# Router scores by token in one product, and a shift shared by two engines

## The reference, cut to what matters

```python
hp = modulate(xp, norm2_g[l], mp[3], mp[4])      # rmsnorm(x) * (1 + scale) + shift
...
scores = jax.nn.sigmoid((t @ router_w).astype(jnp.float32))       # 384 tokens x 16 experts
sel = scores + router_bias.astype(jnp.float32)
...
hid = swiglu(jnp.einsum('td,edf->tef', t, w_in))
routed = jnp.einsum('tef,efd->td', hid * gates[..., None].astype(hid.dtype), w_out)
shared = swiglu(t @ sh_in) @ sh_out
```

## Time and profile before

| what | us |
|---|---|
| median of three runs | 1160.81 |
| lowest and highest of them | 1158.30, 1163.59 |
| the profiled execution | 1160.04 |
| its span in the trace | 1158.2 |

### The profile page before, as it was taken

The page is one execution under the profiler, slowest core; times in us unless marked ns, Lnnn a source line. Parts: engine busy times, 40 slices in busy tenths (PEclk is TensorE's granted clock), DMA queues, the critical chain, the costliest instruction groups (busy, mean ns, idle before and its releaser), DMA issues.

```text
span 1158.2 us, 16832 instructions
## 1 busy us (share of the span) xinstructions
PE 1065.1 (92%) x5726; PEld 835.6 (72%) x5726; DVE 674.9 (58%) x1124; ACT 644.0 (56%) x1155; POOL 312.5 (27%) x265
## 2 busy tenths in 40 slices
PE   5899998899899999999799999978878989999997
PEld 1785654446857888887499999957767976778885
DVE  1432663434355999996565640177766134798994
ACT  2523432445245887886555452398775424588880
POOL 0520920003202000001436655655556600100000
PEclk9899999999988999999899999998898999899999
DMA  9643527993139999995323333476630304999973
GB/s 385 237 182 145 200 109 284 423 420 132 64 114 358 411 411 411 411 409 199 140 73 113 110 111 143 148 214 188 189 119 1 145 1 161 378 412 410 411 311 128
DMA packets 86368, 266.71 MB, mean 230 GB/s; under 512 B 7329, under 2 KB 39585, under 8 KB 73249
## 3 DMA queue, kind: packets, MB, share of 16 engines
q1 hardware_dynamic: 78496, 243.30, 55.6%
q0 software_dynamic: 2880, 12.58, 2.9%
q10 hardware_dynamic: 4928, 10.01, 2.4%
HBM read 245.68 MB, written 15.47 MB: 225 GB/s over the span
## 4 chain that ended last, share of the span: by engine, by line
PE 71%; ACT 8%; DMA 8%; DVE 7%; POOL 3%; issue 2%; SPq 0%; ACTq 0%; POOLq 0%; DVEq 0%
PE bank L2117 16%; PE bank L2118 16%; PE bank L2119 16%; PE bank L2141 3%; PE bank L2401 3%; POOL wlo L736 2%; PE bank L2203 2%; ACT seg L1349 2%; PE bank L2659 2%; DMA h_blk<-h_rows,tok_of 2%; DMA modb<-modb 1%; PE bank L2376 1%; ACT whi L883 1%; DMA rowb<-acs_rows 1%; DMA modw<-wide_mods 1%
## 5 line engine op out<-in xcount | busy, mean ns | idle before, releaser
L736 POOL TENSOR_TENSOR wlo<-raw,whi 128x512 fp32r<-128x512 f32 x152 | 201.0, 1356 | 264.7 <-ACT whi L883 258.9
L2117 PE MATMUL bank<-hhi,whi 128*128 128x384 f32 (+1 forms) x504 | 176.9, 351 | 12.9 <-DVE hlo L1471 9.5
L2118 PE MATMUL bank<-hlo,whi 128*128 128x384 f32 (+1 forms) x504 | 173.3, 344 | 0.0
L2119 PE MATMUL bank<-hhi,wlo 128*128 128x384 f32 (+1 forms) x504 | 173.0, 343 | 0.0
L1849 DVE TENSOR_TENSOR wlo<-raw_more,whi 128x1024 fp32r<-128x1024 f32 x108 | 128.7, 1222 | 14.4 <-ACT whi L1146 12.9
L1849 DVE TENSOR_TENSOR wlo<-raw,whi 128x1024 fp32r<-128x1024 f32 x108 | 128.2, 1221 | 10.3 <-ACT whi L1146 8.1
L1146 ACT CAST whi<-raw_more 128x1024 fp32r<-128x1024 f32 x108 | 111.5, 1049 | 29.6 <-PE bank L2119 25.4
L1146 ACT CAST whi<-raw 128x1024 fp32r<-128x1024 f32 x108 | 111.5, 1053 | 22.6 <-PE bank L2119 12.3
L2117 PE MATMUL bank<-whi,blk_hi 128*128 128x512 f32 x288 | 115.1, 400 | 0.0
L2118 PE MATMUL bank<-wlo,blk_hi 128*128 128x512 f32 x288 | 113.8, 395 | 0.0
L2119 PE MATMUL bank<-whi,blk_lo 128*128 128x512 f32 x288 | 113.7, 395 | 0.0
(11 more groups left out here) (355 smaller groups left out, 1996.6 us busy)
## 6 DMA issues: line engine op xcount, KB each, us to landing
raw<-stream SPq DMA_DIRECT2D x56, 1024.0 KB, 4.8
raw<-experts SPq DMA_DIRECT2D x108, 512.0 KB, 11.4
raw_more<-experts SPq DMA_DIRECT2D x108, 512.0 KB, 11.3
modw<-wide_mods SPq DMA_DIRECT2D x37, 1024.0 KB, 12.5
rowb<-acs_rows SPq DMA_DIRECT2D x48, 256.0 KB, 5.2
shared<-shared SPq DMA_DIRECT2D x6, 1024.0 KB, 6.1
h_next<-h_blk SPq DMA_DIRECT2D x9, 512.0 KB, 10.6
y_rows<-y_sb ACTq DMA_DIRECT2D x9, 512.0 KB, 6.7
```

Source lines behind the costliest of these rows:

```text
L736: ins = pool.tensor_tensor(wlo[:, q % SPL, w], raw[:, pos % RAW, w], whi[:, q % SPL, w].bitcast(F32), ALU.subtract)
L2117: pe.matmul(dst, whi_, xhi_, start=first, stop=False)
L2118: pe.matmul(dst, whi_, xlo_, start=False, stop=False)
L2119: return pe.matmul(dst, wlo_, xhi_, start=False, stop=last)
```

## The change

The job `router` and its result are gone. The job `scores` now does the router's products the other way round: for each chunk of 128 features and each of the three tiles of 128 tokens, the tokens (128 x 128 of `hn`) are stationary and the router's weights (16 columns) are moving. The 24 products gather in one bank as 128 tokens by 3 x 16 scores, and ACT takes the sigmoid of that straight into `rt`. The three small transposes, the sigmoid into `score_rows`, the copy into `rt` and the buffer `score_rows` are removed, and one job less goes through the banks. The scaling and shifting of the odd chunks moves from ACT to DVE, between and after the `scaled_x` instructions; ACT keeps the even chunks. Each engine counts on its own semaphore (`h_even`, `h_odd`), and PE waits for the chunk's own. `h_ready` remains for the other two norms.

```diff
     def moe(layer):
...
-        add([f"norm{2 * layer + 1}", f"router{layer}"] + tok[:2] + [f"scores{layer}"] + tok[2:] +
+        add([f"norm{2 * layer + 1}", f"scores{layer}"] + tok +
...
-        score_rows = mm.put("score_rows", [NTOK])
...
+        h_even, h_odd = sem("h_even"), sem("h_odd")
...
-                ins.then_inc(h_ready, 1)
+                ins.then_inc(h_even if which else h_ready, 1)
...
-                for kc in range(KC):
+                for kc in range(0, KC, 2):
                     norm_affine(phase, kc)
                 act.dma_start(kmoe[:, :], inp["kmoe"]).then_inc(kmoe_in, 16)
-                n = JOB[f"router{layer}"]
+                n = JOB[f"scores{layer}"]
                 finished(act, n)
-                took(act.activation(score_rows[0:NEXP, :], bk(n)[0:NEXP, 0:NTOK], ACT.Sigmoid), n)
+                took(act.activation(rt[:, 0, :], bk(n)[:, 0:TILES * NEXP], ACT.Sigmoid), n)
 
                 for i in range(2 * TILES):
-                    if i == 2:
-                        n = JOB[f"scores{layer}"]
-                        finished(act, n)
-                        took(act.copy(rt[:, 0, :], bk(n)[:, 0:TILES * NEXP]), n)
...
+                dve.wait_ge(gain_ready, 2 * (phase + 1))
+
+                def affine(kc):
+
+                    dve.wait_ge(xr_ready, KC * phase + kc + 1)
+                    for cls, (a, e) in enumerate(CLASSES):
+                        ins = dve.tensor_scalar(hn[:, kc, a:e], hn[:, kc, a:e],
+                                                gain[:, phase, 2 * kc + cls:2 * kc + cls + 1],
+                                                modcol(layer, 3, kc, cls), ALU.mult, ALU.add)
+                    ins.then_inc(h_odd, 1)
+
                 for kc in range(KC):
                     scaled_x(kc)
+                    if kc >= 2 and kc % 2 == 0:
+                        affine(kc - 1)
+                affine(KC - 1)
...
-                n = JOB[f"router{layer}"]
-                dst = opened(n)
+                dst = opened(JOB[f"scores{layer}"])
                 for kc in range(KC):
-                    pe.wait_ge(h_ready, KC * phase + kc + 1)
-                    ins = pe.matmul(dst[0:NEXP, 0:NTOK], v("router", kc * NEXP, NEXP), hn[:, kc, :],
-                                    start=kc == 0, stop=kc == KC - 1)
+                    pe.wait_ge(h_odd if kc % 2 else h_even, KC // 2 * layer + kc // 2 + 1)
+                    for t in range(TILES):
+                        ins = pe.matmul(dst[:, t * NEXP:(t + 1) * NEXP], hn[:, kc, t * P:(t + 1) * P],
+                                        v("router", kc * NEXP, NEXP), start=kc == 0 and t == 0, stop=kc == KC - 1,
+                                        skip_group_check=True)
                 ins.then_inc(jobs_done, 1)
 
                 for i in range(2 * TILES):
-                    if i == 2:
-                        n = JOB[f"scores{layer}"]
-                        dst = opened(n)
-                        taken(pe, JOB[f"router{layer}"])
-                        for t in range(TILES):
-                            ins = pe.transpose(dst[:, t * NEXP:(t + 1) * NEXP], score_rows[0:NEXP, t * P:(t + 1) * P],
-                                               k("ident")[0:NEXP, 0:NEXP])
-                        ins.then_inc(jobs_done, 1)
```

More of the change, by code:

```diff
@@ L942, in norm_hi @@
                     if kc % 2:
-                        act.wait_ge(h_ready, KC * phase + kc)
+                        act.wait_ge(h_ready, KC * (phase // 2) + kc)
                         act.copy(hhi[:, kc - 1, :], hn[:, kc - 1, :]).then_inc(hhi_ready, 1)
@@ L1465, in norm @@
                         if d % 2:
-                            dve.wait_ge(h_ready, KC * phase + d + 1)
+                            dve.wait_ge(h_ready, KC * (phase // 2) + d + 1)
                             step(dve.tensor_copy(hhi[:, d, :], hn[:, d, :]))
```

## The result

Over six runs each, the changed kernel took 1170.65 us (1169.23 to 1174.97) and the kernel before 1158.59 (1156.48 to 1163.59): ratio 1.0098, 95% interval 1.0080 to 1.0116, so 9 to 13 us slower. The profiled execution took 1169.30 with a span of 1167.5; before it was 1160.04 and 1158.2. Where the 9.3 us between the spans went can be read stage by stage.

A forecast was written before the change was run, and what follows sets the result against it. PE's chain was taken as the bound, its clock limiting layer 0's router products. Layer sums of +4.2 and +6.2 us, together +10.4 on the profiled 1160.04, gave 1170.4 us; the range was 1159 to 1175.

The forecast's parts named there:

- the case that I held likeliest: Turned products all at 0.50, clock recovering during the transposes behind them: 1170.4 us, likeliest case spanning 1168 to 1174, chance 0.72.
- products turned round: Router, each layer: 48 matmuls at 0.50 take 10.2 us, against 8.17 and 6.86 before: +2.0 and +3.3 us.
- the clock's recovery: Work behind the router starts at 0.50; the clock returns after a mean 5.0 us, losing 2.5 us a layer.
- small transposes: Three small transposes leave PE's path in each layer: -0.3 us each.
- bank in layer 1: Layer 1's loop: its first product waits for DVE's read of the last shared job, now in bank 0: +0.7 us.
- shared shift: Before the router's products: DVE shifts odd chunks, input over 2 us earlier, worth nothing because PE at 0.50 covers it.
- downstream: Counts, lists, gather and loop behind the router: nothing found that takes the delay up again.
- the plain reading that a busy PE runs fast: First rival, router's products: by busy share alone the new stream raises the clock within them; 1159.7 us, chance 0.14.
- the five stretches that I averaged: Stretches at 0.50 from PE's first work to the clock's rise: 5.78, 5.98, 6.21, 3.12 and 3.92 us, mean 5.0.
- The rival that transposes don't bring the clock back: Behind the router: only the shared product restores the clock, +3.0 us a layer on top, 1176.4 us, chance 0.08.
- The condition that I named: Router's products with PE at 1.00, 0.64 us a chunk: there the earlier input would be worth what it was made for.

The follow-up runs named there:

- wide columns: The changed kernel with the router's 16 moving columns repeated eight times to 128, same weight loads: 1163.45 us, ratio 1.0028 to the kernel before.
- warm start: The changed kernel with five dense products of 384 columns added while PE waits for the norm: 1167.63 us, ratio 1.0060 to the kernel before.
- the turned-only one: The changed kernel with ACT shifting all eight chunks again, so only the products are turned: 1174.26 us, ratio 1.0122 to the kernel before.
- the one with the wait in the loop: The changed kernel with PE's wait for bank 0 moved behind the block count's reading and loop set-up: 1170.94 us, ratio 1.0085 to the kernel before.

## Why the prediction was right, and where it was not

The forecast of 1170.4 us is within 0.3 of the median, and the case that I held likeliest is the one that came. But part of that is luck. The six runs of the kernel before had a median 1.5 us below the profiled execution from which I counted, so by the medians the change costs 12.1 us and not 10.4. And the terms were off in both directions (profile after less profile before):

| term | predicted, us | measured, us |
|---|---|---|
| products turned round, layer 0 and 1 | +2.0, +3.3 | +0.7, +3.5 |
| the clock's recovery, layer 0 and 1 | +2.5, +2.5 | +1.3, +1.3 |
| small transposes | -0.3, -0.3 | -0.3, -0.3 |
| bank in layer 1 | +0.7 | +3.1 |
| shared shift | 0 | 0 |
| downstream | 0 | +1.1 in layer 0's loop |
| sum | +10.4 | +10.4 (spans +9.3) |

The products of layer 0 and the recovery came out 3.7 us cheaper than priced, the bank and the loop 3.5 dearer, and these cancelled.

**The products' clock: right.** From 2.36 us of lists with five columns I took it that a stream of loads with 16 columns would not hold the upper clock, against the plain reading that a busy PE runs fast. Layer 1 shows 0.50 throughout, and the pair of wide columns and warm start shows that the columns are the cause. The price of 0.212 us an instruction measured 10.39 / 48 = 0.216. In layer 0 the profiled execution was still at 1.00 for the first 1.6 us, which the sum had not allowed for; three of the experiments with 16 columns had all of it at 0.50, 10.39 us, one of them without the shared shift. So layer 0's +1.7 is the least of the four kernels with 16 columns and no warm start.

**The recovery: right in kind, too large.** The rise came 3.0 us into the transposes, near the lowest of the five stretches that I averaged: 4.19 us for the transposes against 24 x 0.119 = 2.9, so 1.3 us. The one stretch of transposes alone that I had, 3.38 us at 0.50, was nearer than their mean of 5.0, and I had left it out. The rival that transposes don't bring the clock back is refuted as a rule by both layers of the changed kernel. But transposes at 0.50 for 5.20 us to the last are there too, in layer 1 of the warm-started kernel and in layer 0 of the turned-only one and of the one with the wait in the loop. The Trainium skill, "TensorE: Matmul & The Clock Gate", Part 4, says that full clock doesn't engage for transposes; the traces of the five kernels with 16 columns show it engaging 2.8 to 3.4 us into them in seven stretches and not within 5.2 us in the three just named.

**The bank: the mis-sized term.** I priced the wait at DVE's 0.56 us and a hand-over, and did not list what is queued behind it on PE: the load of the block count and the loop's set-up, which were hidden before and now run after the wait. That is 2.02 us of idle time, and behind it the loop's first nine products ran at 0.50 (1003.90 to 1007.20, which loses 1.65 us). Together that is 0.6 more than the +3.06 that the stretch lost; the rest came back within it. The two experiments that remove the wait, or move it behind the set-up, take layer 1's loop back to within 0.2 us of before.

**The shared shift: right.** Alone it is worth 1.0005 (0.9988 to 1.0022), since PE's clock covers it. The condition that I named, PE at 1.00, is the one under which it pays: 15.3 to 13.7 us in the stage of both layers. The price of 0.6 us a chunk on DVE measured 0.67, and `hn` was complete at 323.2 for a forecast of 323.0.

**Downstream: wrong.** "I find nothing that takes the delay up again" left out that layer 0's loop waits for the experts' data in its first pass, and that this pass goes with the length of PE's list. It was 1.1 us longer here, and some 1.1 us elsewhere came back.

## What to carry to other kernels

A product with many stationary loads and few moving columns can be busy without a gap and still leave PE at half its clock, as 16 columns did here; turn the operands so that the moving side stays long, or stretch it, and cost the work behind it at the lower clock too. An idle wait ahead of a short stage on PE is a place for throw-away dense products, which pay only together with a faster supply: here 0.45% with both, and nothing that the median shows with either. Before a wait moves or appears, list what its engine has queued behind it, loads of registers and loop set-up included.

## What the runs showed that I had not expected

Eight times the moving columns made the same 24 products shorter, from 8.89 to 5.60 us in layer 0 and from 10.39 to 7.17 in layer 1, and the kernel 7 us faster; the stage gained 4.8 us a layer where I had expected 3.5 at most. And 28 more instructions for PE in each layer, in a time when it is idle, go with 2.7 us more in layer 0's loop, some 30 us later (40.62 against 37.92 with the shared shift alone).
